# Operands and most of the arena start 32 bytes further in a two-block fp32 kernel

## The chip, the cores and the metric

One core of a Trainium2 chip runs the whole program. The metric is the device time of one execution in microseconds, the median of the runs shown. Lower is better.

## The reference, cut to what matters

The reference runs two transformer blocks, one after the other, on 256 tokens of width 2048 in fp32, batch 1.

```python
x = first_block(x, c, ...)      # depth 1: HGRN2 + dilated attention + conv, merged by gates, then squared-relu MLP
x = second_block(x, c_2, ctx_2, ...)  # depth 1: mLSTM + differential attention with 256 context tokens, then conv MLP
```

In the first block:

```python
h = rms_norm(x, mix_norm_pre[l]) * (1.0 + sc1) + sh1
... = split_cols(h @ w_in[l], IN_SPLITS)
gates = jax.nn.sigmoid(h @ w_gate[l] + b_gate[l])
merged = gates0 * (ya @ w_a_out[l]) + gates1 * (yb @ w_b_out[l]) + gates2 * (yc @ w_c_out[l])
x = x + g1 * rms_norm(merged @ w_o[l], mix_norm_post[l])
y = jnp.square(jax.nn.relu(h @ w_up[l])) @ w_down[l]
```

The second block has the same shape with its own mixers, and a feed-forward part whose up-projection has 2 x 5632 columns, is convolved over three tokens and gated. Almost all of the arithmetic is products of a 256-token activation with fp32 weights. Each block's modulation vectors come from the product of one row with a matrix of 2048 x 12288.

## The kernel before, in words

**The weight stream.** All weights lie in one list of tiles of 128 partitions x 16 x 128 floats (1 MB), in the order in which they are used. SyncE issues one DMA for each tile as its slot comes free (line 455), into 4 slots of `sb_raw`; during the first 48 tiles there are 8 slots, 4 of them in the arena. Each tile of a matrix product is one block `b`.

**High and low parts.** A product in fp32 precision is made of three products of fp32r parts. ScalarE rounds a tile to its high part (`split_high`, line 539) and VectorE subtracts that to get the low part (`split_low`, line 1779). Both go to `sb_parts`, which is `[P, 2, 2, KT, P]`: two buffers by `b % 2`, high and low, 16 tiles of 128 columns.

**The products.** TensorE takes a weight tile of `sb_parts` as the stationary operand and 256 columns (the tokens) of an activation operand as the moving one, 16 tiles of the contraction into one PSUM bank. `product` issues the high weights with the operand's high and low half (line 1040, 32 matmuls of 256 columns), then the low weights with the operand's high half (line 1049, 16 matmuls). `gemm_parts`, used for the down-projections, takes both halves as one moving operand of 512 columns (line 1076, 16 matmuls) and adds the low weights with 256 columns (line 1079, 16 matmuls). In some sections the roles are exchanged and the moving operand is the weight tile (`gemm_tokens`). Line 1207 is the same product, tile by tile in the first stage, where the modulation vectors are still being made beside it (line 1189, on TensorE, and lines 1752 to 1760 and 1890, on VectorE).

**The memory.** After the small tensors lies `arena`, `[P, 37120]` floats, in which the regions of all stages overlap by hand: `region(at, ...)` is a view at element `at`. The fp32r operands (`opH`, `opU1`, `opW` and so on) need another type, so `operand` allocates a padding of `at` floats and the operand behind it, and frees both before the arena itself is allocated at the same start; operand and region with the same `at` share memory. The residual `xT` is the region at 0. All operands lie at element 4096 or later, at multiples of 512 floats. As built, `sb_raw` starts at byte 4,224 of a partition, `sb_parts` at 36,992 and the arena at 80,064.

**The sections.** The start (modulation of block one beside the first product), the input projections in sixes and eights of blocks with the mixers' small matmuls between them, gates and branches, merge, `w_o`, then four quarters of up and down projection; the second block likewise, with `m_*` and `d_*` as projections, `w_out_a`, `w_out_b`, and four quarters `up2_q` (22 blocks, 48 matmuls each) and `down2_q` (16 blocks). VectorE also convolves in the first block: `conv_taps` (line 1941) reads the padded input `upad[:, t, j:j + S]` at tap offset j and adds into `cy`. `scaled_tile` (line 1834) reads `xT` and writes the arena. `keep_warm` (line 1173) issues matmuls of `ones` with itself.

The order is written out on each engine by hand, with semaphores; nothing in it depends on an address.

Of the kernel before, what the change touches and what calls it, by code (L numbers as in the profile page):

```python
# [5 lines left out]
F32 = mybir.dt.float32  # L6
# [5 lines left out]
F32R = mybir.dt.float32r  # L12

P = 128
# [137 lines left out]
def two_blocks_kernel(nc, stream, x_t, ctx_t, vec_d, const_d, lvl_mask_d, ident_d, rel_bias, c_rows, scratch, x_keep, out_t):  # L152
    with ExitStack() as ctx:
        def sb(name, shape, dt=F32):
            return ctx.enter_context(nc.sbuf_tensor("sb_" + name, shape, dt))
# [15 lines left out]
        small = sb("small", [P, 128])  # L171
        ARENA = 37120

        def operand(name, at, *dims):
            with nc.sbuf_tensor("pad_" + name, [P, at], F32), nc.sbuf_tensor("op_" + name, [P, *dims], F32R) as t:
                return t

        def paired(name, at, *dims):  # L180


            *lead, tiles = dims
            t = operand(name, at, *lead, tiles, 2, S)
            if lead:
                return t[:, :, :, :, :].rearrange("p w k a s -> p w a k s")
            return t[:, :, :, :].rearrange("p k a s -> p a k s")

        opH = paired("h", 4096, KT)
        opYa = operand("ya_hi", 25600, 8, S), operand("ya_lo", 20480, 8, S)  # L190
        opYb = operand("yb_hi", 27648, 2, S), operand("yb_lo", 30208, 2, S)
        opYc = operand("yc_hi", 31232, 6, S), operand("yc_lo", 28672, 6, S)
        opG = paired("merged", 12288, KT)
# [3 lines left out]
        max_rows = rstd[0:8, :]  # L197
        opYd = operand("yd", 12288, 2, 8, S)
        opU2 = paired("up2", 12288, UP2)
        arena = sb("arena", [P, ARENA])  # L200
        G = [ctx.enter_context(nc.psum_tensor(f"gemm{i}", [P, 512], F32)) for i in range(4)]
        M = [ctx.enter_context(nc.psum_tensor(f"mix{i}", [P, 512], F32)) for i in range(4)]

        def region(at, *dims):
            n = 1
            for d in dims:
                n *= d
            assert at + n <= ARENA, (at, dims)
            flat = arena[:, at:at + n]
            if len(dims) == 1:  # L210
                return flat
            names = "abc"[:len(dims)]
            return flat.rearrange(f"p ({' '.join(names)}) -> p {' '.join(names)}", **dict(zip(names, dims)))

        def v(name, i=0, n=1):
            return vec[:, VEC[name] + i:VEC[name] + i + n]

        xT = region(0, KT, S)

        sq0 = region(12288, KT, S)  # L220
        hf0 = region(12288, KT, S)
        onehot, bmask, brow = region(20480, BPITCH), region(20864, BPITCH), region(34560, BPITCH)
        relb = region(21632, 12)
# [2351 lines left out]
```

## Time and profile before

| | us |
|---|---|
| median of 3 runs | 3195.09 |
| lowest and highest run | 3189.89, 3201.64 |
| the profiled execution | 3204.8 |
| its span, first to last instruction | 3202.9 |

| engine | busy share of the span |
|---|---|
| TensorE, matmuls | 97% |
| TensorE, weight loads (PEld) | 92% |
| VectorE | 74% |
| ScalarE | 42% |

Matmuls are pipelined: a record's duration, from start to the end of its last result, overlaps the next one's, so the time that a matmul costs is the distance of two starts. Over a window without idle time that is the window divided by the number of matmuls that start in it. Weight loads run beside the matmuls and have an engine row of their own.

### The profile page before, as it was taken

The numbers are of one execution on the slowest core, as the hardware profiler recorded it, in microseconds if no ns is written. First come the engines' busy times: TensorE is split into PE (matmuls) and PEld (weight loads), VectorE is DVE, ScalarE is ACT, GpSimd is POOL, SyncE is SP. The second block draws the span as 40 slices with busy tenths as digits, with TensorE's granted clock in tenths as the row PEclk, the third lists the DMA queues.
The fourth block names the chain that finished last, engine by engine and source line by source line (L and its number), as shares of the span: only waits on it lengthen the run. The fifth ranks groups of instructions, "written<-read, shape, count | busy, mean of one in ns | idle before, by whom it ended". The sixth has DMA issues, their size and how long they took to land.

```text
span 3202.9 us, 55394 instructions
## 1 busy us (share of the span) xinstructions
PE 3119.9 (97%) x23974; PEld 2952.1 (92%) x23974; DVE 2370.9 (74%) x2843; ACT 1335.0 (42%) x1459; POOL 1.8 (0%) x10
## 2 busy tenths in 40 slices
PE   7999999999999999999999999999999999999997
PEld 5899999999999999998988999989889989898996
DVE  5799876687887789989978765544767666766766
ACT  3333344434444443333364333422465444343444
POOL 0000000000000000000000000000000000000000
PEclk9999999999999999999999999999999999999999
DMA  9864444588894887777755763354343475655753
GB/s 401 324 218 158 171 149 150 189 332 332 312 370 154 300 310 263 268 256 291 289 185 198 288 247 144 139 214 158 119 153 134 172 260 192 228 207 189 257 177 126
DMA packets 106417, 722.62 MB, mean 226 GB/s; under 512 B 11677, under 2 KB 15389, under 8 KB 27197
## 3 DMA queue, kind: packets, MB, share of 16 engines
q1 hardware_dynamic: 100368, 703.64, 59.5%
q10 hardware_dynamic: 5806, 15.43, 1.6%
q8 instruction: 190, 3.11, 0.4%
q14 instruction: 53, 0.43, 0.0%
HBM read 712.41 MB, written 6.55 MB: 224 GB/s over the span
## 4 chain that ended last, share of the span: by engine, by line
PE 87%; DVE 7%; DMA 3%; ACT 2%; issue 1%; ACTq 0%; DVEq 0%
PE gemm L1040 38%; PE gemm L1049 19%; PE gemm L1076 11%; PE gemm L1079 6%; DMA sb_raw<-stream 3%; DVE sb_parts L1779 2%; ACT sb_parts L539 1%; PE mix L1040 1%; PE mix L1291 1%; PE mix L1569 1%; DMA sb_arena<-x_t 1%; DVE sb_arena L1834 1%; PE mix L1049 1%; PE gemm L1207 1%; DVE sb_arena L1890 1%
## 5 line engine op out<-in xcount | busy, mean ns | idle before, releaser
L539 ACT ACTIVATE sb_parts<-sb_raw 128x2048 fp32r<-128x2048 f32 (+2 forms) x489 | 899.3, 1842 | 1508.6 <-PE gemm L1049 973.5
L1779 DVE TENSOR_TENSOR sb_parts<-sb_raw,sb_parts 128x2048 fp32r<-128x2048 f32 (+2 forms) x489 | 1072.3, 2194 | 304.3 <-PE gemm L1049 148.3
L1040 PE MATMUL gemm<-op_h,sb_parts 128*128 128x256 f32 x7232 | 884.7, 279 | 1.0 <-ACT sb_parts L539 0.6
L1040 PEld LDWEIGHTS gemm<-op_h,sb_parts 128*128 128x128 f32 x7232 | 861.3, 188 | 2.5 <-ACT sb_parts L539 1.0
L1049 PE MATMUL gemm<-op_h,sb_parts 128*128 128x256 f32 x3616 | 459.4, 279 | 0.0
L1049 PEld LDWEIGHTS gemm<-op_h,sb_parts 128*128 128x128 f32 x3616 | 438.6, 188 | 0.2 <-DVE sb_parts L1779 0.2
L1076 PE MATMUL gemm<-op_up,sb_parts 128*128 128x512 f32 x1728 | 422.2, 395 | 11.9 <-DVE op_up L2408 11.7
L1076 PEld LDWEIGHTS gemm<-op_up,sb_parts 128*128 128x128 f32 x1728 | 318.4, 190 | 75.4 <-DVE op_up L2408 13.5
L1079 PEld LDWEIGHTS gemm<-op_up,sb_parts 128*128 128x128 f32 x1728 | 222.2, 191 | 10.6
L1760 DVE CUSTOM_DVE_ANT_0 sb_raw<-sb_raw,sb_arena,sb_vec 128x2048 f32<-128x2048 f32 x96 | 224.4, 2349 | 1.2
L1079 PE MATMUL gemm<-op_up,sb_parts 128*128 128x256 f32 x1728 | 224.5, 281 | 0.0
L1040 PE MATMUL gemm<-op_hw,sb_parts 128*128 128x256 f32 (+1 forms) x992 | 174.3, 333 | 0.3 <-ACT sb_parts L539 0.3
L1040 PEld LDWEIGHTS gemm<-op_hw,sb_parts 128*128 128x128 f32 x992 | 150.3, 188 | 20.1 <-ACT sb_parts L539 0.5
L1752 DVE CUSTOM_DVE_ANT_0 sb_raw<-sb_raw,sb_arena,sb_vec 128x2048 f32<-128x2048 f32 x64 | 149.8, 2346 | 0.0
L2399 DVE SCALAR_TENSOR_TENSOR sb_arena<-gemm,sb_vec,sb_arena 128x255 f32<-128x255 f32 x88 | 42.5, 483 | 135.8 <-ACT sb_arena L991 135.8
L1040 PEld LDWEIGHTS gemm<-sb_parts,op_hw 128*128 128x128 f32 x1024 | 121.0, 191 | 3.4 <-ACT sb_parts L539 1.6
L1040 PE MATMUL gemm<-sb_parts,op_hw 128*128 128x256 f32 x1024 | 122.3, 282 | 1.5 <-ACT sb_parts L539 1.5
L1049 PE MATMUL gemm<-op_hw,sb_parts 128*128 128x256 f32 (+1 forms) x496 | 89.6, 333 | 0.0
L1814 DVE TENSOR_TENSOR sb_arena<-gemm,sb_arena 128x256 f32<-128x256 f32 x96 | 40.6, 423 | 63.8 <-PE gemm L1079 63.8
L1049 PEld LDWEIGHTS gemm<-op_hw,sb_parts 128*128 128x128 f32 x496 | 75.8, 188 | 9.9
L2138 DVE TENSOR_TENSOR sb_arena<-sb_arena 128x256 f32<-128x256 f32 x64 | 27.1, 423 | 65.5 <-ACT sb_arena L790 65.5
L1759 DVE CUSTOM_DVE_ANT_0 sb_arena<-sb_raw,sb_arena,sb_vec 128x2048 f32<-128x2048 f32 x32 | 75.1, 2346 | 0.0
(360 smaller groups left out, 3386.6 us busy)
## 6 DMA issues: line engine op xcount, KB each, us to landing
sb_raw<-stream SPq DMA_DIRECT2D x597, 1024.0 KB, 5.0
sb_raw<-stream SPq DMA_DIRECT2D x64, 704.0 KB, 4.2
sb_arena<-stream SPq DMA_DIRECT2D x14, 1024.0 KB, 8.3
sb_arena<-stream SPq DMA_DIRECT2D x10, 768.0 KB, 8.0
sb_raw<-stream SPq DMA_DIRECT2D x6, 768.0 KB, 7.4
sb_arena<-c_rows ACTq DMA_DIRECT2D x3, 1024.0 KB, 7.4
bias_rows<-sb_arena ACTq DMA_DIRECT2D x1, 2304.0 KB
sb_arena<-x_t ACTq DMA_DIRECT2D x4, 512.0 KB, 19.2
```

What stands on the lines that cost most here:

```text
L539: act.activation(parts[:, b % 2, 0, 0:kt, :], slot_of(slot)[:, 0:kt, :], ACT.Copy).then_inc(hi_ready, 1)
L1040: ins = pe.matmul(out, l, r, start=(opens and i == 0 and x is xh), stop=False, skip_group_check=True)
L1049: ins = pe.matmul(out, l, r, start=False, stop=(i == len(terms) - 1), skip_group_check=True)
L1076: pe.matmul(bank(b)[:, :], parts[:, b % 2, 0, k, :], both, start=(k == 0), stop=False, skip_group_check=True)
L1079: ins = pe.matmul(bank(b)[:, 0:S], parts[:, b % 2, 1, k, :], op[:, 0, k, :], start=False, stop=(k == kt - 1), skip_group_check=True)
L1207: ins = pe.matmul(out[:, i * S:(i + 1) * S], w, opH[:, p, k, :], start=(k == i == part == p == 0), stop=(k == KT - 1 and part == 1), skip_ ...
L1752: dve.tensor_tensor_reduce(w, w, c1_row, 1.0, v("b_ada", a), ALU.mult, ALU.add, mod1[:, a:a + 1])\
L1759: step(dve.tensor_tensor_reduce(products, w, cctx_row, 1.0, v("b_mod", a), ALU.mult, ALU.add, mod2[:, 1, a:a + 1]))
L1760: dve.tensor_tensor_reduce(w, w, c2_row, 1.0, v("b_mod", a), ALU.mult, ALU.add, mod2[:, 0, a:a + 1])\
L1779: dve.tensor_tensor(parts[:, b % 2, 1, 0:kt, :], slot_of(slot)[:, 0:kt, :], parts[:, b % 2, 0, 0:kt, :].bitcast(F32), ALU.subtract).then_i ...
L1814: step(dve.tensor_tensor(acc, bank(b)[:, 0:S], acc, ALU.add))
L2399: step(dve.scalar_tensor_tensor(y[:, 1:S], src[:, 0:S - 1], w0, y[:, 1:S], ALU.mult, ALU.add))
```

## The change

Everything in the arena at element 4096 or later starts 8 floats, 32 bytes, further: the padding ahead of each fp32r operand is 8 floats longer, each region view from 4096 on is moved by 8, and the arena is 8 floats longer. Regions below 4096 (`xT` and some small tables of the second block) stay, as do `sb_raw`, `sb_parts` and all small tensors ahead of the arena. Regions and operands that share memory still do. No instruction is added, removed or moved.

```diff
+        def placed(at):
+            return at + (8 if at >= 4096 else 0)
+
         def operand(name, at, *dims):
-            with nc.sbuf_tensor("pad_" + name, [P, at], F32), nc.sbuf_tensor("op_" + name, [P, *dims], F32R) as t:
+            with nc.sbuf_tensor("pad_" + name, [P, placed(at)], F32), nc.sbuf_tensor("op_" + name, [P, *dims], F32R) as t:
                 return t
...
-        arena = sb("arena", [P, ARENA])
+        arena = sb("arena", [P, placed(ARENA)])
...
             assert at + n <= ARENA, (at, dims)
-            flat = arena[:, at:at + n]
+            flat = arena[:, placed(at):placed(at) + n]
```

## Rows read from the trace of the kernel before

**Rows 1.** The page: busy us, share of the span and instructions of each engine.

```profile
PE 3119.9 (97%) x23974; PEld 2952.1 (92%) x23974; DVE 2370.9 (74%) x2843; ACT 1335.0 (42%) x1459; POOL 1.8 (0%) x10
```

**Rows 2.** The page: chain that ended last, by engine and by line.

```profile
PE 87%; DVE 7%; DMA 3%; ACT 2%; issue 1%; ACTq 0%; DVEq 0%
PE gemm L1040 38%; PE gemm L1049 19%; PE gemm L1076 11%; PE gemm L1079 6%; DMA sb_raw<-stream 3%; DVE sb_parts L1779 2%; ACT sb_parts L539 1%; PE mix L1040 1%; PE mix L1291 1%; PE mix L1569 1%; DMA sb_arena<-x_t 1%; DVE sb_arena L1834 1%; PE mix L1049 1%; PE gemm L1207 1%; DVE sb_arena L1890 1%
```

**Rows 3.** Windows: busy us and instructions of each engine, clock, DMA share, GB/s.

```profile
0.00:140.00 140.00, 112.12 (x1161) 97.34 (x1162) 87.19 (x122) 48.59 (x66) 1.78 (x10) 1.00 0.95 387
860.00:960.00 100.00, 97.88 (x824) 96.88 (x823) 82.12 (x73) 44.85 (x52) 0.00 (x0) 1.00 0.93 351
```

**Rows 4.** The chain within 860 to 985 us, in order of time, its longest pieces.

```profile
886.70 7.63 DMA sb_raw<-stream
896.31 2.30 DVE sb_parts L1779
898.63 7.43 DMA sb_raw<-stream
...
932.84 8.23 DMA sb_raw<-stream
```

**Rows 5.** Windows inside up2_1, up2_2, up2_3: PE, PEld, DVE, ACT, POOL.

```profile
2630.00:2740.00 110.00, 110.00 (x973) 110.00 (x972) 76.48 (x92) 50.56 (x52) 0.00 (x0) 1.00 0.53 186
2815.00:2925.00 110.00, 110.00 (x936) 110.00 (x936) 73.51 (x87) 48.28 (x49) 0.00 (x0) 1.00 0.51 181
3008.00:3118.00 110.00, 110.00 (x973) 110.00 (x972) 76.83 (x93) 50.04 (x50) 0.00 (x0) 1.00 0.52 183
```

**Rows 6.** Groups by line, first in 2630:2740, then 2815:2925 (count, busy, mean ns).

```profile
L1040 PE MATMUL gemm<-op_h,sb_parts 128*128 128x256 f32 x653 | 77.4, 276 | 0.0
...
L1040 PE MATMUL gemm<-op_h,sb_parts 128*128 128x256 f32 x632 | 77.7, 279 | 0.0
```

**Rows 7.** TensorE's timeline in a down-projection: start us, us, instructions merged.

```profile
1093.70 1.98 PE L1079 MATMUL gemm<-op_up,sb_parts 128*128 128x256 f32 x16
1095.51 3.82 PE L1076 MATMUL gemm<-op_up,sb_parts 128*128 128x512 f32 x16
1099.17 2.04 PE L1079 MATMUL gemm<-op_up,sb_parts 128*128 128x256 f32 x16
...
1104.73 1.98 PE L1079 MATMUL gemm<-op_up,sb_parts 128*128 128x256 f32 x16
...
1110.20 2.05 PE L1079 MATMUL gemm<-op_up,sb_parts 128*128 128x256 f32 x16
```

**Rows 8.** Groups by line over the span: the products with op_h.

```profile
L1040 PE MATMUL gemm<-op_h,sb_parts 128*128 128x256 f32 x7232 | 884.7, 279 | 1.0 <-ACT sb_parts L539 0.6 <-DVE sb_arena L1926 0.5
L1049 PE MATMUL gemm<-op_h,sb_parts 128*128 128x256 f32 x3616 | 459.4, 279 | 0.0
```

**Rows 9.** The same view: products with op_merged and op_yd.

```profile
L1040 PE MATMUL gemm<-op_merged,sb_parts 128*128 128x256 f32 x512 | 63.1, 280 | 1.1 <-ACT sb_parts L539 0.9
L1040 PE MATMUL gemm<-op_yd,sb_parts 128*128 128x256 f32 x256 | 33.0, 288 | 3.4 <-ACT sb_arena L960 3.4
L1049 PE MATMUL gemm<-op_merged,sb_parts 128*128 128x256 f32 x256 | 32.5, 279 | 0.0
L1049 PE MATMUL gemm<-op_yd,sb_parts 128*128 128x256 f32 x128 | 16.4, 279 | 0.0
```

**Rows 10.** Single lines on VectorE: duration ns min/median/max, first and last start.

```profile
L1941 DVE SCALAR_TENSOR_TENSOR sb_arena<-sb_arena,sb_vec x180: 467/480/486, 151.1 to 342.5; 128x256 f32<-128x256 f32 x180
L1834 DVE SCALAR_TENSOR_TENSOR sb_arena<-sb_arena,sb_small,sb_rstd x64: 476/480/489, 33.1 to 2441.1; 128x256 f32<-128x256 f32 x64
```

**Rows 11.** DMA issues within 0 to 125 us: KB each, median us to landing.

```profile
sb_raw<-stream SPq DMA_DIRECT2D x21, 1024.0 KB, 8.4
sb_arena<-stream SPq DMA_DIRECT2D x14, 1024.0 KB, 8.3
```

**Rows 12.** A window of matmuls with 512 columns (section m_k), TensorE alone.

```profile
1755.00:1785.00 30.00, 30.00 (x132) 1.00 0.90 341
```

**Rows 13.** A window of keep_warm matmuls (line 1173 alone): PE, PEld.

```profile
959.00:963.20 4.20, 4.02 (x36) 3.82 (x35) 1.00 0.55 222
```

## What 32 bytes more do to the time, predicted blind

> **What bounds the kernel now.** I read the busy table first, then the chain that ended last, then the groups by line, and only then short windows. TensorE is busy for 97% of the span and the other engines are well below it [rows 1]; the chain is 87% TensorE, with the weight products of lines 1040, 1049, 1076 and 1079 as 74% of the span [rows 2]. So the question is whether 32 bytes change what one matmul takes. Only two stretches are set by something else: the first 140 us, where the DMA engines are 95% busy [rows 3], and the merge stage near 860 to 960 us, where the chain lies on weight loads from HBM and on VectorE [rows 4].
>
> **How a matmul of 256 columns is paced.** TensorE runs with no idle time in long windows, so window divided by count is the time of one. In one quarter of the last feed-forward section 110 us hold 973 matmuls, 113.0 ns each; in the next quarter, same lines, same tiles, same addresses, the same 2.4 GHz clock, 110 us hold 936, 117.5 ns each; in the last quarter 973 again [rows 5]. VectorE, ScalarE and the DMA engines are as busy in the 117.5 ns quarter as in its neighbours (0.51 and 0.53, 0.52 of the DMA engines), so it isn't their traffic. The duration of the single record tells the two levels apart: 276 ns at the short pitch, 279 ns at the long one [rows 6]. The time is therefore quantised: 113.3 ns is 272 cycles of 2.4 GHz, 117.9 ns is 283. The stage around 1100 us shows what chooses. There runs of 16 matmuls with 512 columns (line 1076) alternate with 16 of 256 columns (line 1079), and the 256-column runs last 1.98, 2.04, 1.98, 2.05 us in turn [rows 7], with nothing waited for. 1.98 against 2.04 is the same 4 ns a matmul. So the level hangs on the phase at which a run is entered, and then stays: a phase lock between the two streams that TensorE reads from memory, the moving operand and the weights of the next matmul, whose loads run beside it (PEld is 92% busy).
>
> By the lines' groups most matmuls have the long pitch. Lines 1040 and 1049 with op_h are 7232 and 3616, mean 279 ns [rows 8]; of them the two short-pitch quarters hold 22 x 48 each, 2,112, which leaves 8,736 long ones. Half of the 1,728 of line 1079 are long (864), so are op_merged (512 and 256), op_yd (256 and 128) [rows 9], and, as an estimate from the like groups of the other branch operands, op_hw and line 1207, about 2,500 more. That is some 13,000 long and, of a total near 18,500, some 5,000 short.
>
> **The change, part by part.** It adds no instruction, wait, byte or dependence, and moves nothing in any queue; every order in the program is as before. What differs is one number: each op_* operand and each arena region from element 4096 on starts 8 floats later. As the program is laid out, the weight tiles sb_parts begin at byte 36,992 and the arena at byte 80,064 of a partition, both multiples of 64; every operand's offset is a multiple of 2,048 bytes, every tile's of 512. So before, moving operand and weights both start on a multiple of 64 bytes in every product; after, the operand starts 32 past one and the weights don't. sb_raw, sb_parts and xT stay.
>
> VectorE and ScalarE: no row shows an arena access that is 32 bytes off by itself, but line 1941 is near it. It reads the padded convolution input at tap offsets 1 to 30, so its first operand starts at every multiple of 4 bytes of a 64-byte unit in turn while its accumulator stays on one; 180 such instructions last 467 to 486 ns, median 480 [rows 10]. Bound: -2.7% to +1.3%, taken as nothing. The aligned xT reads of line 1834 last the same 480 [rows 10]. Even +1.3% on VectorE's 2,371 us is 31 us of an engine that has 26% to spare, and about a tenth of it, 3 us, would lie on the chain (VectorE is 7% of it [rows 2]).
>
> DMA: the operands aren't loaded by DMA. 24 stream tiles land in the arena in the first 125 us. Today tiles that go to sb_raw take 8.4 us to land and those to sb_arena 8.3 [rows 11], though their starts differ by an odd multiple of 64 bytes. A 32-byte start isn't shown. If each arena tile cost 10% more, 0.8 us, with about three in flight, it would be 24 x 0.8 / 3 = 6 us; if it cost as much less, -6 us. I take nothing, by the equal rows.
>
> TensorE: this is the term. A price from below: if the long pitch is where the two streams meet at the same part of a 64-byte unit, 32 bytes take them apart and every long pitch becomes the short one: 13,000 x 4.5 ns = 58 us. Some of it does not count. The 768 matmuls of op_merged lie in the merge stage, which waits for loads anyway (3.5 us). That leaves 55 us. A price from above: if it locks everything into the long pitch, 5,000 x 4.5 = 23 us more. The 2,448 matmuls with 512 columns take 30 us / 132 = 227 ns on either side of this [rows 12], more than twice 113.0 and less than twice 117.5, so they hold the middle between the levels; going to twice 113.0 gives 3 us, to twice 117.5 costs 19.
>
> A rule to weigh: the Trainium skill, "SBUF — State Buffer", section "Specifications (TRN2)", gives 16-byte lines, with a penalty for each new line. 32 bytes are two whole lines, so by that rule an operand crosses as many lines as before and nothing changes. The same skill, "TensorE: Matmul & The Clock Gate", part 2, says that loading the next weights takes nothing from a running matmul's reads, because they have ports of their own. The trace shows two levels at one clock for the same work [rows 5], which that rule doesn't explain. The time by these rules is that of the first rival below.
>
> **The rivals.** The forecast: the shift parts the streams; the long pitch goes over to the short one, 276 ns. For it: 70% of the matmuls have the long pitch where both streams start alike; the short one is exactly 272 = 17 x 16 cycles, and 16 cycles is what 64 bytes of a moving operand last, so 64 bytes is a natural period and 32 is its middle. Against: both levels occur at the same addresses, so the address alone doesn't choose.
>
> Rival 1, no effect: the lock depends on time alone, or on a period of 32 bytes or less. For it: the two levels at one address [rows 5], and line 1941, which doesn't feel the phase [rows 10]. The time is then the present one, 3195, with some quarters changing levels: one quarter is 1,056 x 4.5 = 4.8 us, and the runs shown of before, 3189.9 to 3201.6, spread by two or three of those.
>
> Rival 2, slower: the shift closes the short pitch. The moving operand of 1,024 bytes then touches 17 units of 64 bytes and not 16. If each matmul pays for the extra unit only what today separates the levels, the short 5,000 become long and the wide ones too: 23 + 19 = 42 us at the worst, 23 at the least, 3218 to 3237. It decides wherever the engine never idles, so from 140 us on. For it: the operand's start is the thing that the long pitch might hang on, too. Against: a majority is long already, so less is left to lose.
>
> Rival 3, more than the levels: the present short pitch still holds a stall. Idle-filling matmuls of 128 columns with all 128 weights (line 1173) come at 4.2 us / 36 = 117 ns with the gaps at their edges, 4.02 / 36 = 112 busy [rows 13]: a full weight load is what they share with the product lines, and it looks like a floor of about 112. Reaching it gives 18,500 x 1 ns = 19 us on top of 55, and on the wide ones 2,448 x (227 - 224) = 8 us: 3113.
>
> **How the numbers follow.** The profiled execution took 3204.8 us with a span of 3202.9, 9.7 over the median 3195.1; the levels' share is of that execution, and I apply the difference to the median: 3195.1 - 55 = 3140 us. Chances: forecast 0.38, rival 3 0.08, rival 1 0.32, rival 2 0.22. The likeliest case's own range is 3120 to 3165 (a part of the long pitches goes over, or the wide ones too). The range over all cases leaves out about one in ten at either end: low 3110 just under rival 3, high 3218 at the lower price of rival 2. About 0.5% (16 us) is what a measurement of this kernel can tell from no change; forecast and rival 3 lie beyond it on the one side, rival 2 on the other: faster 0.45, same 0.33, slower 0.22.
>
> **What the profile after would show.** Right: the groups of lines 1040 and 1049 with op_h at 276 ns, all three windows [rows 5] with 973, line 1079's runs all at 1.98 us. Rival 1: again a mixture of 276 and 279, whichever section holds which. Rival 2: 279 or more everywhere, the wide ones over 227 ns. Rival 3: under 113 ns in a window with no idle. VectorE's 480 ns, the 8.3 us of arena tiles and the 95% of the first 140 us should stay; if they moved, the parts I took at nothing are wrong. The forecast falls as a whole if TensorE's rate changes by something that isn't a step between the two levels, or if the freed time is given back to waits for the high parts (line 539), which today is only 1.2% of the chain [rows 2].

## The result, and the profile after

The change made the kernel slower: 3266.8 us (3266.7 to 3267.0 in four runs) against 3198.4 us before (3195.1 in the three runs shown above and 3201.9 in a fourth), ratio 1.0207 with a 95% interval of 1.0178 to 1.0237. In absolute terms that is 68 us more, where I had forecast 55 us less. The profiled execution took 3267.0 us, its span 3265.2, which is 62.3 us over the span of before.

The page after, busy time of the engines and the chain by engine (lines are 6 higher than before: 1046 is 1040, 1055 is 1049, 1082 is 1076, 1085 is 1079):

```profile
PE 3189.2 (98%) x23974; PEld 3011.6 (92%) x23974; DVE 2371.9 (73%) x2843; ACT 1334.5 (41%) x1459; POOL 1.8 (0%) x10
...
PE 91%; DVE 5%; DMA 1%; ACT 1%; issue 1%; ACTq 0%; DVEq 0%
```

TensorE is busy 69.3 us longer than in [rows 1], with the same number of instructions; VectorE and ScalarE differ by 1.0 and 0.5 us. So the time went where the forecast said that the only term lies. The groups of the products, the same view as [rows 8]:

```profile
L1046 PE MATMUL gemm<-op_h,sb_parts 128*128 128x256 f32 x7232 | 907.0, 282 | 1.0 <-ACT sb_parts L545 0.5 <-DVE sb_arena L1932 0.5
L1055 PE MATMUL gemm<-op_h,sb_parts 128*128 128x256 f32 x3616 | 470.6, 282 | 0.0
L1082 PE MATMUL gemm<-op_up,sb_parts 128*128 128x512 f32 x1728 | 427.3, 397 | 11.6 <-DVE op_up L2414 11.6
```

A record lasts 282 ns, which is neither 276 nor 279. The products with op_h cost 22.3 and 11.2 us more, the wide ones (512 columns) of the down-projections 5.1 us, against this line of the page of before:

```profile
L1076 PE MATMUL gemm<-op_up,sb_parts 128*128 128x512 f32 x1728 | 422.2, 395 | 11.9 <-DVE op_up L2408 11.7
```

The three quarters again, TensorE alone, the windows moved to where the quarters now lie (as [rows 5]; columns are window, busy us and count, clock, DMA share, GB/s):

```profile
2675.00:2785.00 110.00, 110.00 (x919) 1.00 0.48 176
2865.00:2975.00 110.00, 110.00 (x919) 1.00 0.49 177
3062.00:3172.00 110.00, 110.00 (x919) 1.00 0.48 174
```

All three hold 919, at the full granted clock. Divided out that is 119.7 ns for one, but these counts hold the two or three matmuls that were already running when the window opened, so a quotient reads 0.3 to 0.4 ns low. The distance from the start of one block of 48 matmuls to the start of the next has no such error. First two blocks of up2_1 and two of up2_2 before, then two of up2_1 after:

```profile
2700.34 3.79 PE L1040 MATMUL gemm<-op_h,sb_parts 128*128 128x256 f32 x32
...
2705.78 3.79 PE L1040 MATMUL gemm<-op_h,sb_parts 128*128 128x256 f32 x32
...
2820.02 3.93 PE L1040 MATMUL gemm<-op_h,sb_parts 128*128 128x256 f32 x32
...
2825.67 3.93 PE L1040 MATMUL gemm<-op_h,sb_parts 128*128 128x256 f32 x32
```

```profile
2680.46 4.00 PE L1046 MATMUL gemm<-op_h,sb_parts 128*128 128x256 f32 x32
...
2686.22 4.00 PE L1046 MATMUL gemm<-op_h,sb_parts 128*128 128x256 f32 x32
```

That is 5.44 us or 113.3 ns a matmul at the short pitch, 5.65 or 5.66 us, 117.8 ns, at the long one, and 5.76 us or 120.0 ns after the change. From here on pitches are taken this way; the 113.0, 117.5 and 227 ns of the prediction are the quotients. Followed through the whole trace, 177 blocks of op_h have another right behind them; 42 of these were at 113.3 before and 132 at 117.8, and after the change 174 are at 120.0 (the other three in each trace are first blocks of a section and last longer). Both levels of before are gone, and the one that stands in their place is above both and just as steady. The runs of the down-projection that were 1.98 and 2.04 us in turn [rows 7] now all last 2.08, and the wide ones 3.89 against 3.82:

```profile
1105.14 3.89 PE L1082 MATMUL gemm<-op_up,sb_parts 128*128 128x512 f32 x16
1108.87 2.08 PE L1085 MATMUL gemm<-op_up,sb_parts 128*128 128x256 f32 x16
1110.79 3.89 PE L1082 MATMUL gemm<-op_up,sb_parts 128*128 128x512 f32 x16
1114.53 2.08 PE L1085 MATMUL gemm<-op_up,sb_parts 128*128 128x256 f32 x16
```

From start to start 16 wide ones take 3.73 us, 233 ns each, where they took 3.66 us, 229 ns each, in the same section before ([rows 7], 1095.51 to 1099.17). The two things that I had put at nothing stayed there:

```profile
L1947 DVE SCALAR_TENSOR_TENSOR sb_arena<-sb_arena,sb_vec x180: 473/478/485, 152.1 to 347.6; 128x256 f32<-128x256 f32 x180
L1840 DVE SCALAR_TENSOR_TENSOR sb_arena<-sb_arena,sb_small,sb_rstd x64: 470/477/486, 33.5 to 2482.4; 128x256 f32<-128x256 f32 x64
```

```profile
sb_raw<-stream SPq DMA_DIRECT2D x21, 1024.0 KB, 8.8
sb_arena<-stream SPq DMA_DIRECT2D x14, 1024.0 KB, 8.2
```

```profile
0.00:140.00 140.00, 115.38 (x1154) 100.12 (x1155) 86.35 (x120) 48.46 (x66) 1.77 (x10) 0.98 0.95 387
```

The first fence is VectorE, as [rows 10], 478 and 477 ns for 480; the second the DMA issues of the first 125 us, as [rows 11], 8.2 us for 8.3 into the shifted arena (8.8 for 8.4 into `sb_raw`, which was not shifted, so single transfers scatter by more than the shift could be seen to do). The third is the first 140 us, as [rows 3]: 0.95 of the DMA engines and 387 GB/s, both as before. TensorE is busy there for 115.4 us where it was 112.1, at a mean granted clock of 0.98 for 1.00, so a part of these 3.3 of the 69.3 us is the clock's.

### The profile page after: what moved, and what is told of

The parts are those of the page before. It is cut to its first block, busy times and chain, and to the rows that moved or that the text cites. A ratio compares the mean times of both kernels' runs of the same rounds, so it can differ in the third digit from the quotient of the medians.

```text
span 3265.2 us, 55394 instructions
## 1 busy us (share of the span) xinstructions
PE 3189.2 (98%) x23974; PEld 3011.6 (92%) x23974; DVE 2371.9 (73%) x2843; ACT 1334.5 (41%) x1459; POOL 1.8 (0%) x10
## 4 chain that ended last, share of the span: by engine, by line
PE 91%; DVE 5%; DMA 1%; ACT 1%; issue 1%; ACTq 0%; DVEq 0%
PE gemm L1046 40%; PE gemm L1055 20%; PE gemm L1082 12%; PE gemm L1085 6%; PE mix L1046 1%; DVE sb_parts L1785 1%; PE mix L1297 1%; PE mix L1575 1%; DMA sb_arena<-x_t 1%; PE gemm L1213 1%; DVE sb_arena L1840 1%; PE mix L1055 1%; ACT sb_parts L545 1%; PE mix L1156 1%; PE gemm L1641 0%
## 5 line engine op out<-in xcount | busy, mean ns | idle before, releaser
L1046 PE MATMUL gemm<-op_h,sb_parts 128*128 128x256 f32 x7232 | 907.0, 282 | 1.0 <-ACT sb_parts L545 0.5
L1046 PEld LDWEIGHTS gemm<-op_h,sb_parts 128*128 128x128 f32 x7232 | 883.0, 188 | 2.4 <-ACT sb_parts L545 1.0
L1055 PE MATMUL gemm<-op_h,sb_parts 128*128 128x256 f32 x3616 | 470.6, 282 | 0.0
L1055 PEld LDWEIGHTS gemm<-op_h,sb_parts 128*128 128x128 f32 x3616 | 449.2, 188 | 0.1
L1046 PE MATMUL gemm<-op_hw,sb_parts 128*128 128x256 f32 (+1 forms) x992 | 178.7, 337 | 0.3 <-ACT sb_parts L545 0.3
L1046 PE MATMUL gemm<-sb_parts,op_hw 128*128 128x256 f32 x1024 | 124.8, 283 | 0.7 <-ACT sb_parts L545 0.7
L1055 PE MATMUL gemm<-op_hw,sb_parts 128*128 128x256 f32 (+1 forms) x496 | 91.8, 337 | 0.0
```

Of the source, the lines that this page charges most:

```text
L1046: ins = pe.matmul(out, l, r, start=(opens and i == 0 and x is xh), stop=False, skip_group_check=True)
L1055: ins = pe.matmul(out, l, r, start=False, stop=(i == len(terms) - 1), skip_group_check=True)
```

## The experiments

Two theories stood after the result. **Theory A**: the moving operand's own start counts; off a multiple of 64 bytes it reads 17 units for 16, as my rival 2 had it. **Theory R**: only the distance between the two streams counts, the moving operand's start less the start of the weight tile that is being loaded beside it, modulo some power of two. Before the change that distance is 80,064 - 36,992 = 43,072, which is 64 modulo 128 (and modulo 256); after it, 96.

The shifts below are made by the same function `placed` as in the change; the cuts write the number out where the runs have a constant `SHIFT`. Where a shift isn't a multiple of 32 bytes, the operand is a view into a slightly larger allocation, because the allocator starts tensors at multiples of 32.

### Weights moved as well

```diff
+        sb("gap", [P, 8])
         parts = sb("parts", [P, 2, 2, KT, P], F32R)
+        sb("gap2", [P, 24])
         ident = sb("ident", [P, P])
...
+            return at + (8 if at >= 4096 else 0)
```

> The weight tiles (sb_parts) start 32 bytes past a multiple of 64 as the operands do in the changed kernel; small tensors and arena keep their place modulo 128. Theory A, the start of the moving operand against a 64-byte unit costs time by itself: as the changed kernel or more, about 3267 us, pitch 120 ns in the op_h products, no 276 ns level. Theory R, only the distance of the two streams counts: they start alike again as in the kernel before, so about 3198 us, with levels 276 and 279 ns and a spread of several us between runs.

Measured 3185.2 us (nine runs, 3178.7 to 3194.4) against 3200.4 before on that chip, ratio 0.9953 [0.9929, 0.9977]. A window in up2_1:

```profile
2632.00:2732.00 100.00, 100.00 (x885) 1.00 0.52 186
```

That is the count of the short pitch, 113.3 ns, though both streams start 32 bytes off a multiple of 64. Theory A is out: the start by itself costs nothing. It is even a little better than before, which theory R in its form modulo 128 didn't foresee; modulo 256 the distance here is 192.

### Weights moved alone

```diff
+        sb("gap", [P, 8])
         parts = sb("parts", [P, 2, 2, KT, P], F32R)
+        sb("gap2", [P, 24])
         ident = sb("ident", [P, P])
```

> Only the weight tiles (sb_parts) start 32 bytes past a multiple of 64; operands and arena where the kernel before has them (modulo 128). Theory A: the moving operand is aligned in all products but those in which the weight tile is the moving one (lines 1040 and 1049 with gemm<-sb_parts, some 2,200 matmuls), so about 3198 us plus 2,200 x 3 ns = 7 us: 3205. Theory R: the streams lie 32 bytes apart, so as the changed kernel, about 3267 us and 120 ns.

Measured 3250.9 us, ratio 1.0154 [1.0116, 1.0191]. The same window of the same quarter:

```profile
2670.00:2770.00 100.00, 100.00 (x845) 1.00 0.50 179
```

From block to block that is 118.7 ns. The two gaps move operands and arena by 128 bytes. Moving them by 128 bytes with the weights in place costs nothing (3183.6 us, below), so this loss comes from the weight tiles' place. Theory A had 3205. Theory R had 3267; the direction is right, the size is 3/4 of it.

### Other distances: 64 and 16 bytes

```diff
-            return at + (8 if at >= 4096 else 0)
+            return at + (16 if at >= 4096 else 0)    # the other run: 4
```

> The change with 16 floats, 64 bytes, in place of 8. If 64 bytes is the period, both theories expect the time before, about 3198 us, with the 276 and 279 ns levels. If the place modulo 128 counts, another time: the operands now start alike with the weights modulo 128, before they were 64 apart.

> The change with 4 floats, 16 bytes, in place of 8. Theory A with a unit of 64 bytes: a moving operand off the unit by any amount touches 17 units, so about 3267 us. With a unit of 32 bytes the 32-byte shift would have been free, so that is out already. Theory R, distance of the streams: a time of its own, between or outside 3198 and 3267, since the distance is a quarter of the unit.

Measured 3250.8 us (1.0154 [1.0117, 1.0191]) with 64 bytes and 3249.5 us (1.0151 [1.0114, 1.0188]) with 16. So 64 bytes is not a period, against what I had reasoned from 16 cycles, and "start alike modulo 128" is as bad as most others.

### One weight buffer alone

```diff
-        parts = sb("parts", [P, 2, 2, KT, P], F32R)
+        wide = sb("parts", [P, 2, 2 * KT * P + 8], F32R)
+        parts = wide[:, :, 0:2 * KT * P].rearrange("p w (h k c) -> p w h k c", h=2, k=KT)
+        sb("gap2", [P, 16])
```

> Operands and arena as before modulo 128; of the two weight buffers the second alone starts 32 bytes further (distance 32, that of the run in which both buffers did). Theory R: within one run the blocks take two paces in turn by the buffer, those with even b at 113 or 118 ns and those with odd b at about 118.5 ns on average without a fixed level, and the whole lies between 3198 and 3251, near 3225 us. If it is an effect of the whole layout (DMA, other engines, the place of the instructions): all blocks pace alike.

Measured 3215.7 us, ratio 1.0053 [1.0035, 1.0071]. The operands are 192 (modulo 256) past the first buffer and 160 past the second. TensorE's timeline in up2_1, block after block, with the two instructions that make the next weight tiles beside it:

```profile
2700.16 4.00 PE L1042 MATMUL gemm<-op_h,sb_parts 128*128 128x256 f32 x32
...
2702.33 2.29 DVE L1781 TENSOR_TENSOR sb_parts<-sb_raw,sb_parts 128x2048 fp32r<-128x2048 f32 x1 [0.21 <-DVE sb_arena L2402]
...
2704.00 2.08 PE L1051 MATMUL gemm<-op_h,sb_parts 128*128 128x256 f32 x16
...
2705.92 3.80 PE L1042 MATMUL gemm<-op_h,sb_parts 128*128 128x256 f32 x32
...
2708.01 2.29 DVE L1781 TENSOR_TENSOR sb_parts<-sb_raw,sb_parts 128x2048 fp32r<-128x2048 f32 x1 [0.21 <-DVE sb_arena L2402]
...
2709.55 1.98 PE L1051 MATMUL gemm<-op_h,sb_parts 128*128 128x256 f32 x16
...
2711.37 4.00 PE L1042 MATMUL gemm<-op_h,sb_parts 128*128 128x256 f32 x32
```

The 48 matmuls of one block take 2705.92 - 2700.16 = 5.76 us, 120.0 ns each; those of the next 5.45 us, 113.5 each, and so on by turns. The section starts with b = 385 and its blocks with odd b, the ones that read the second, shifted buffer, are the slow ones. Same operand, same engines' work beside it (VectorE's subtraction takes 2.29 us beside either), same run: the buffer that the weights are read from sets the pace. Within the slow block both parts have the pitch of 120.0 ns (32 matmuls in 3.84 us, 16 in 1.92 us), though VectorE subtracts for only 2.29 of the 5.76 us. That settles that neither the layout of the other tensors nor VectorE nor the DMA is the cause. I had expected 118.5 for the shifted buffer; it held 120.0.

### 128, 112 and 8 bytes

```diff
-            return at + (8 if at >= 4096 else 0)
+            return at + (32 if at >= 4096 else 0)    # the other runs: 28, 2
```

> The change with 32 floats, 128 bytes. Theory R with a period of 128 bytes (weights and operands 64 apart modulo 128, as before): the time before, about 3198 us, levels 276 and 279 ns. If the period is longer than 128 bytes: another time, about 3250 us, as the shifts by 16, 32 and 64 bytes gave.

> The change with 28 floats, 112 bytes, so that operand and weights are 48 apart modulo 128. Theory R, in the form that only the distance 64 lets the pitch lock: about 3250 us, pitch 118 to 120 ns. If the distances below 64 lock as well as 64 does (only those above 64 are bad): about 3198 us or less.

> The change with 2 floats, 8 bytes: distance 72 modulo 128, half a line of 16 bytes beside the good one. If the units that collide are lines of 16 bytes and a start inside one costs a 17th or 65th access: about 3250 us. If the lock is to 64 give or take some bytes: about 3198 us.

128 bytes: 3183.6 us (nine runs, 3174.6 to 3194.8), ratio 0.9957 [0.993, 0.9984]; 112 bytes: 3255.2, 1.0182 [1.0129, 1.0236]; 8 bytes: 3274.9, 1.0244 [1.019, 1.0298], the worst of all. The good distance is sharp: half a 16-byte line beside it costs more than any larger step. With 128 bytes all three quarters have the count of the short pitch:

```profile
2608.00:2718.00 110.00, 110.00 (x973) 1.00 0.53 186
2790.00:2900.00 110.00, 110.00 (x973) 1.00 0.54 193
2978.00:3088.00 110.00, 110.00 (x973) 1.00 0.54 190
```

But its groups show that 128 isn't the period either:

```profile
L1044 PE MATMUL gemm<-op_h,sb_parts 128*128 128x256 f32 x7232 | 866.6, 278 | 1.2 <-ACT sb_parts L543 0.7 <-DVE sb_arena L1930 0.5
...
L1080 PE MATMUL gemm<-op_up,sb_parts 128*128 128x512 f32 x1728 | 426.6, 396 | 11.6 <-DVE op_up L2412 11.6
...
L1044 PE MATMUL gemm<-sb_parts,op_hw 128*128 128x256 f32 x1024 | 124.9, 283 | 0.8 <-ACT sb_parts L543 0.8
```

The last kind before, in which the weight tile is the moving operand:

```profile
L1040 PE MATMUL gemm<-sb_parts,op_hw 128*128 128x256 f32 x1024 | 122.3, 282 | 1.5 <-ACT sb_parts L539 1.5
```

Against before, the op_h products of this line gained 18.1 us (884.7 [rows 8]), while the wide ones lost 4.4 and those with the weight tile as the moving operand lost 2.6. In the last kind the roles are exchanged, so the distance has the other sign: 64 before, 192 after, is for them 192 before and 64 after. Both kinds do better at 192 and less well at 64, and that fits a period of 256 bytes. For the exchanged kind, though, 64 isn't a good place at all: it takes 124.9 us there, 124.8 after the change (distance 160 for them) and 123.4 with a shift of 160 bytes (distance 32).

### 256, 192 and 160 bytes

```diff
-            return at + (8 if at >= 4096 else 0)
+            return at + (64 if at >= 4096 else 0)    # the other runs: 48, 40
```

> The change with 64 floats, 256 bytes. If the period is 256 bytes: the kernel before in everything, 3199 us with runs between 3180 and 3209, op_h pitch a mixture of 113 and 118, wide matmuls 229 ns, weight tile as moving operand 115. If it is 128 and the 16 us between the 128-byte shift and before came from elsewhere, then as that: about 3184 us, wide 233, 118.

> Distance 0 modulo 256, both streams alike (before it was 64, after 96). If the period is 128, as with the shift of 64 bytes (distance 128): 3251 us, op_h pitch 118.7 on average. If the sign that I forecast holds in some form (starting alike is the worst case): more than any so far, over 3275.

> Distance 224 modulo 256, which is 32 on from the best one (192) as the change is 32 on from 64. Theory: only 64 and 192 lock; about 3250 to 3270 us, pitch 118.5 to 120, no 113 level.

256 bytes: 3203.5 us against 3197.0, ratio 1.0023 [1.0005, 1.0042], runs from 3196.2 to 3211.1, that is the kernel before, or 0.2% over it. 192 bytes (distance 0): 3255.3, 1.0189 [1.0148, 1.0231]. 160 bytes (distance 224): 3244.3, 1.0155 [1.0113, 1.0196]. The groups with 256 bytes are those of before again, the wide ones and the exchanged ones with them:

```profile
L1080 PE MATMUL gemm<-op_up,sb_parts 128*128 128x512 f32 x1728 | 419.1, 393 | 11.7 <-DVE op_up L2412 11.7
...
L1044 PE MATMUL gemm<-sb_parts,op_hw 128*128 128x256 f32 x1024 | 121.7, 281 | 1.4 <-ACT sb_parts L543 1.4
```

At distance 0 all is even, and yet not good. A window in up2_1, and the groups:

```profile
2668.00:2778.00 110.00, 110.00 (x919) 1.00 0.49 175
```

```profile
L1044 PE MATMUL gemm<-op_h,sb_parts 128*128 128x256 f32 x7232 | 907.1, 283 | 1.0 <-ACT sb_parts L543 0.5 <-DVE sb_arena L1930 0.5
...
L1080 PE MATMUL gemm<-op_up,sb_parts 128*128 128x512 f32 x1728 | 418.8, 392 | 11.7 <-DVE op_up L2412 11.7
```

The same count as after the change, and again 120.0 ns in 174 blocks of op_h, but the wide ones 418.8 us, no worse than before (422.2). Starting alike is thus bad, though not "more than any so far".

### A version by operand

```diff
+        MOVED = {"hw": 64, "up1": 64, "up2": 64}
+
+        def placed(at):
+            return at + (96 if at >= 20480 else 32 if at >= 4096 else 0)
...
-            with nc.sbuf_tensor("pad_" + name, [P, at], F32), ...
+            with nc.sbuf_tensor("pad_" + name, [P, at + MOVED[name] if name in MOVED else placed(at)], F32), ...
```

> Each operand at the distance that its products did best at, now read modulo 256: op_h, op_merged and the branch operands 192 past the weights (arena from 4096 on 32 floats further, from 20480 on 96), op_hw and op_up 64 past them (64 floats further, 256 bytes), where the wide matmuls took 229 ns against 233 and the products with the weight tile as the moving operand 115 against 118. From the run with a shift of 128 bytes, 3184 us: 2,430 wide x 4 ns and 2,170 x 3 ns less, 16 us: about 3168 us, faster than both kernels. If the distances don't add up operand by operand: 3184 to 3200.

Measured 3185.5 us (twelve runs, 3173.8 to 3196.2) against 3197.0, ratio 0.9967 [0.9947, 0.9987]. It beats both kernels, but is no better than the plain shift of 128 bytes (the two intervals largely overlap), and misses its 3168.

```profile
L1044 PE MATMUL gemm<-op_h,sb_parts 128*128 128x256 f32 x7232 | 877.4, 279 | 1.2 <-ACT sb_parts L543 0.7 <-DVE sb_arena L1930 0.5
L1053 PE MATMUL gemm<-op_h,sb_parts 128*128 128x256 f32 x3616 | 455.0, 279 | 0.1
L1080 PE MATMUL gemm<-op_up,sb_parts 128*128 128x512 f32 x1728 | 418.4, 392 | 11.7 <-DVE op_up L2412 11.7
...
L1044 PE MATMUL gemm<-sb_parts,op_hw 128*128 128x256 f32 x1024 | 122.2, 282 | 1.4 <-ACT sb_parts L543 1.4
```

The wide and the exchanged products got their 8.2 and 2.7 us, as expected. What was lost is in op_h, 877.4 for 866.6 us and 455.0 for 449.6, together the 16 us that were to be gained, at the same distance of 192. The three quarters show it; they are at the long pitch again:

```profile
2600.00:2710.00 110.00, 110.00 (x937) 1.00 0.51 183
2788.00:2898.00 110.00, 110.00 (x936) 1.00 0.51 179
2980.00:3090.00 110.00, 110.00 (x936) 1.00 0.51 179
```

So at 192 both levels still exist. Of 174 blocks of op_h 162 were at the short pitch with the shift of 128 bytes, 99 with weights and operands both moved and 81 here, each in one execution; at 64 it was 42 before and 72 with the shift of 256. A section keeps its level from its second block to its end. What decides which one it enters isn't shown, and neither is whether this version has the short one less often than the plain shift or only had it so in the execution that was profiled.

### All distances together

The last column is the pitch of the op_h products from block to block, in ns, the commonest first.

| distance mod 256 | run | median us | ratio to before | pitch |
|---|---|---|---|---|
| 0 | shift 192 | 3255.3 | 1.0189 | 120.0 |
| 64 | before; shift 256 | 3197 to 3200; 3203.5 | 1; 1.0023 | 117.8, 113.3 |
| 72 | shift 8 | 3274.9 | 1.0244 | 120.3 |
| 80 | shift 16 | 3249.5 | 1.0151 | 118.3, 120.0 |
| 96 | the change | 3266.8 | 1.0207 | 120.0 |
| 128 | shift 64 | 3250.8 | 1.0154 | 118.7 |
| 160 | weights 32 | 3250.9 | 1.0154 | 118.7, 117.3, 120.0 |
| 176 | shift 112 | 3255.2 | 1.0182 | 119.2 |
| 192 | shift 128; both 32 | 3183.6; 3185.2 | 0.9957; 0.9953 | 113.3, 117.8 |
| 224 | shift 160 | 3244.3 | 1.0155 | 118.3 |

Two distances of ten are good, 64 and 192, and the kernel before had one of them. The other eight lie within 1% of each other. What marks the two is the value 113.3, not that there are levels: every distance has its own level or levels, each steady to 0.2 ns.

## Why the prediction was wrong

**Right.** What bounds the kernel and where its time can move: TensorE's pitch alone. That VectorE, ScalarE and DMA don't feel 32 bytes: 477 for 480 ns, 8.2 for 8.3 us. That the two levels belong to the interplay of the two streams, not to the other engines' traffic: the run with one shifted buffer shows it.

**Wrong, the step that decides.** "If the long pitch is where the two streams meet at the same part of a 64-byte unit, 32 bytes take them apart." Three things in it fail. The period isn't 64 bytes (64 bytes of shift gave 3250.8, 256 gave the old time back). Distance 64 wasn't the meeting point but one of the two places, of ten tried, at which the short pitch occurs at all. And I had assumed that the two levels of the trace are the only ones; after the change neither is left, and all of op_h runs at 120.0 ns. So the term of 55 us less was TensorE 69.3 us busier. I read 70% long pitches as a bad place with room to gain, when the presence of 113.3 ns at all was the sign of a good one. That 272 cycles is 17 x 16 carried nothing: 118.3 ns, at 16 and 160 bytes of shift, is 284 cycles of 2.4 GHz, no multiple of 16. My own objection, that both levels occur at the same addresses, was the better reading of [rows 5]: it says that the address doesn't choose between those two, and so that moving it has no reason to favour one. That the level is a phase lock, entered by chance, is still only my name for it.

**Rival 2** had the direction with 0.22 and the wrong mechanism and size. A moving operand that touches 17 units was refuted by moving both streams (3185.2). Its price, 23 to 42 us, took the long pitch as the ceiling. By the measured pitches: 5,000 x (120.0 - 113.3) = 33.5 us, 13,000 x (120.0 - 117.8) = 28.6 us, 2,448 wide ones x (233 - 229) = 9.8 us, together 72 us, where the counts 5,000 and 13,000 are estimates. TensorE's busy time grew by 69.3 and the span by 62.3. The 7 us between these two were waits that the slower TensorE covers: it is idle for 76 us of the span and was for 83. DMA's share of the chain fell from 3% [rows 2] to 1%, and loads are what the merge stage waited for [rows 4]. The price of the wide matmuls was off as well: they started from 229 ns and not 227.

**Rival 1** fell with the time. The rule on lines of the Trainium skill, "SBUF — State Buffer", section "Specifications (TRN2)", taken alone as I took it, would have every shift by whole 16-byte lines free. The runs do not agree: 16, 32, 64, 112, 160 and 192 bytes cost 1.5 to 2.1%. The Trainium skill, "TensorE: Matmul & The Clock Gate", part 2, says that loading the next weights takes nothing from what a running matmul reads. The two are not independent here: moving the weight tiles costs 1.5%, and moving one of two buffers slows only the blocks that read it. Whether it is reading that is lost, no run shows.

**Rival 3** found nothing: no section of op_h in any run has a pitch under 113.3 ns.

**The range** ended at 3218 because its upper end was the lower price of rival 2, itself bounded by a level seen in the trace. A bound for an unknown mechanism can't be taken from the two values that a known state of it happens to show.

## What to carry to other kernels

Where matmuls reload their weights each time and TensorE never idles, the place of the moving operand relative to the weight tile in a partition is worth 2% here, by steps of a few bytes, and it is no question of alignment of either one. Before touching such a layout, take the pitch from the starts of equal blocks without idle time. A steady pitch says nothing by itself, 120.0 ns is as steady as 113.3; but if some sections are clearly faster than others with the same work, the layout may be one of the few good ones, and here eight of nine other distances lost it (a tensor of 8 floats ahead of the arena is enough for that). Try a few distances over 256 bytes rather than reasoning about one.

## What the hardware showed that I hadn't expected

- The pitch of a 256-column fp32r matmul with its own weight load depends on the distance of the two operands: 113.3 or 117.8 ns at distances 64 and 192, 120.0 at 0 and 96, 118.3 at 224, 118.7 at 128 and in most blocks at 160, all in windows at the full granted clock. The period is 256 bytes as far as two pairs show it: the shift of 256 bytes gives the groups of before, and so do op_up and op_hw moved by 256 bytes in the version by operand.
- A shift of 8 bytes costs 2.4%, more than one of 16, 32 or 64.
- The two widths don't like the same place. The 1,728 wide matmuls take 418.8 us at distance 0, 418.4 to 422.2 in three runs at 64 and 426.2 and 426.6 at 192.
- At the eight other distances the time repeats within 0.1 to 4.1 us (3266.7 to 3267.0 after the change); at 64 and 192 it spreads over 15 to 29 us (before: 3180 to 3209). It fits that there each section enters one of two levels, but only one execution of each kernel was profiled, so the levels of the others aren't seen.
- Why there are such levels, what chooses between two of them, and what in the memory has a period of 256 bytes, stays open. No run here separates banks, lines and the order in which a weight tile is read.
